# Plain fp32 matmuls in place of split fp32r products in a one-core transformer step

## What is computed

```
mod = silu(cond) @ w_mod + b_mod            # 2 conditioning vectors, 2048 x 12288, split into 6 parts
h   = rmsnorm(x) * (1 + sc_m) + sh_m
u   = h @ w_in                              # 384 x 2048 x 5120
m   = concat(A diff attention, B gated recurrence, C neighbourhood attention, D grouped attention)(u)
x   = x + g_m * rmsnorm(m @ w_out)          # 384 x 2048 x 2048
h   = rmsnorm(x) * (1 + sc_f) + sh_f
a,g = split(h @ w_ffn_in)                   # 384 x 2048 x 11264
x   = x + g_f * rmsnorm((silu(g) * a) @ w_ffn_out)   # 384 x 5632 x 2048
```

## Time and profile before

| what | value |
|---|---|
| median of 3 runs | 2067.38 us (2067.26 to 2074.31) |
| profiled execution, its span | 2065.1 us |
| profiled execution, its own time | not given beside the span |
| TensorE busy | 1910.1 us, 92% |
| VectorE busy | 1047.9 us, 51% |
| ScalarE busy | 857.6 us, 42% |
| HBM read | 311.54 MB |
| mean granted TensorE clock over the span | 0.969 of full |

### The profile page before, as it was taken

The page is one execution under the profiler, slowest core; times in us unless marked ns, Lnnn a source line. Parts: engine busy times, 40 slices in busy tenths (PEclk is TensorE's granted clock), DMA queues, the critical chain, the costliest instruction groups (busy, mean ns, idle before and its releaser), DMA issues.

```text
span 2065.1 us, 23115 instructions
## 1 busy us (share of the span) xinstructions
PE 1910.1 (92%) x8491; PEld 1460.6 (71%) x8491; DVE 1047.9 (51%) x1289; ACT 857.6 (42%) x1167; POOL 157.4 (8%) x225
## 2 busy tenths in 40 slices
PE   3889999999996779959999999999999989999995
PEld 1348666666664558848888888888888878888884
DVE  4883675866667743446233332333333345555553
ACT  4663555556555543333232322323223234444542
POOL 2000102410007700000000000000000000000000
PEclk8999999999998889979999999999999999999998
DMA  8873666666654023324333333333333343333321
GB/s 288 318 284 123 232 219 252 224 252 232 247 214 147 6 102 122 122 97 148 123 122 122 133 112 141 122 123 129 118 138 122 122 164 135 129 123 123 123 102 61
DMA packets 45028, 320.91 MB, mean 155 GB/s; under 512 B 5436, under 2 KB 5816, under 8 KB 7144
## 3 DMA queue, kind: packets, MB, share of 16 engines
q1 hardware_dynamic: 41216, 297.95, 39.5%
q0 software_dynamic: 3152, 18.93, 2.7%
q10 hardware_dynamic: 600, 3.21, 0.4%
HBM read 311.54 MB, written 8.52 MB: 155 GB/s over the span
## 4 chain that ended last, share of the span: by engine, by line
PE 83%; DVE 8%; ACT 3%; issue 2%; DMA 2%; DVEq 0%; ACTq 0%; POOL 0%; SPq 0%
PE ps L632 24%; PE ps L634 24%; PE ps L633 24%; DVE wlo L898 3%; PE ps L617 3%; PE ps L618 2%; ACT whi L279 1%; DMA raw<-in_weights 1%; PE ps L645 1%; DVE smalls L1112 1%; DMA rows<-in_state_rglru 1%; PE ps L847 1%; PE ps L773 1%; DVE x_sb L1203 1%; PE ps L796 1%
## 5 line engine op out<-in xcount | busy, mean ns | idle before, releaser
L898 DVE TENSOR_TENSOR wlo<-raw,whi 128x1024 fp32r<-128x1024 f32 x568 | 689.5, 1243 | 743.4 <-ACT whi L279 741.5
L279 ACT ACTIVATE whi<-raw 128x1024 fp32r<-128x1024 f32 x568 | 582.8, 1056 | 788.1 <-PE ps L634 753.1
L632 PE MATMUL ps<-whi,h_hi 128*128 128x512 f32 x1728 | 682.2, 395 | 18.8 <-DVE wlo L898 11.8
L634 PE MATMUL ps<-wlo,h_hi 128*128 128x512 f32 x1728 | 673.8, 390 | 0.0
L633 PE MATMUL ps<-whi,h_lo 128*128 128x512 f32 x1728 | 673.3, 390 | 0.0
L632 PEld LDWEIGHTS ps<-whi,h_hi 128*128 128x128 f32 x1728 | 324.9, 188 | 97.7 <-DVE wlo L898 22.4
L633 PEld LDWEIGHTS ps<-whi,h_lo 128*128 128x128 f32 x1728 | 325.0, 188 | 68.1 <-issue 1.7
L634 PEld LDWEIGHTS ps<-wlo,h_hi 128*128 128x128 f32 x1728 | 324.8, 188 | 68.3
L632 PE MATMUL ps<-whi,j_hi 128*128 128x512 f32 x528 | 209.7, 397 | 5.4 <-DVE j_lo L1253 3.9
L633 PE MATMUL ps<-whi,j_lo 128*128 128x512 f32 x528 | 206.1, 390 | 0.0
L634 PE MATMUL ps<-wlo,j_hi 128*128 128x512 f32 x528 | 206.1, 390 | 0.0
(11 more groups left out here) (204 smaller groups left out, 1033.0 us busy)
## 6 DMA issues: line engine op xcount, KB each, us to landing
raw<-in_weights SPq DMA_DIRECT2D x284, 1024.0 KB, 4.8
x_dram<-x_sb POOLq DMA_DIRECT2D x1, 3072.0 KB, 9.1
x_sb<-x_dram POOLq DMA_DIRECT2D x1, 3072.0 KB, 10.7
out<-x_sb POOLq DMA_DIRECT2D x3, 1024.0 KB, 4.7
x_sb<-in_x_sample ACTq DMA_DIRECT2D x1, 2048.0 KB, 15.0
x_sb<-in_x_sample POOLq DMA_DIRECT2D x1, 2048.0 KB, 9.4
x_sb<-in_x_prompt ACTq DMA_DIRECT2D x1, 1024.0 KB, 5.0
gw<-in_lru_gate_w POOLq DMA_DIRECT2D x4, 256.0 KB, 3.3
```

The lines of the kernel that those rows point to most:

```text
L279: nc.scalar.activation(whi[:, s % RING * 2 + b], raw[:, s, HK * b:HK * b + HK], ACT.Copy)\
L632: nc.tensor.matmul(acc, xh[:, kk + HK * b, xs], wh[:, kk, :], start=(k == 0), stop=False)
L634: ins = nc.tensor.matmul(acc, xh[:, kk + HK * b, xs], wl[:, kk, :], start=False, stop=(k == k_last))
L898: nc.vector.tensor_tensor(wlo[:, s % RING * 2 + b], raw[:, s, HK * b:HK * b + HK], whi[:, s % RING * 2 + b].bitcast(F32), ALU.subtract).th ...
```

## The change

1. All fp32r buffers, splits and their semaphores go. A matmul is plain fp32 on the raw weight tile and on unsplit activations (`hT`, `h3T`, `stat`). ScalarE and VectorE no longer touch weights.
2. `proj_tile` is 12 plain fp32 matmuls: tokens stationary, 512 weight columns moving. It serves the input projection, the output projection and the second FFN product.
3. `mod_tile` has the weights stationary: 16 plain fp32 matmuls, each with a 128x128 block of the tile loaded and two columns moving. The result lies in columns, so `rows_out`, `mod_select` and `cols_out` go; VectorE adds the bias on its way out of PSUM (`mod_out`).
4. The first FFN product has the weights stationary too. A tile is now 128 output columns x 2048 rows (`chunk`), 16 plain fp32 matmuls with 384 token columns moving. The result is already transposed: `h3_transposes` and `ht_out` go, and the work is in 44 pairs of tiles.
5. The ring has 10 tiles, and a slot is free once TensorE has used it. The residual stays in SBUF; both copies through DRAM go.
6. All loops over registers are written out.

```diff
-RAW = 4
-RING = 2
-HK = KG // 2
+RAW = 10
...
-C_F2 = C_F1 + 2 * FFN_N * KG
+C_F2 = C_F1 + 2 * FK
...
@@ sync
-            with sp.Fori(1, N_TILES // RAW) as i:
-                for s in range(RAW):
-
-                    sp.wait_ge(w_lo, i * (2 * RAW) + (2 * (s + 1) - 2 * RAW))
-                    sp.dma_start(raw[:, s].rearrange("p k n -> p (k n)"), wst[i * RAW + s]).then_inc(raw_in[s], 16)
+            for t in range(N_TILES):
+                if t >= RAW:
+                    sp.wait_ge(w_used, t - RAW + 1)
+                sp.dma_start(raw[:, t % RAW].rearrange("p k n -> p (k n)"), wst[t]).then_inc(raw_in[t % RAW], 16)
...
@@ tensor
-            def mod_tile(t, s, kg, bank):
-
-                for b, wh, wl in halves(t, s):
-                    for kk in range(HK):
-                        k = KG * kg + HK * b + kk
-                        nc.tensor.matmul(ps[bank][0:4, :], stat[:, k, :], wh[:, kk, :], start=(k == 0), stop=False)
-                        ins = nc.tensor.matmul(ps[bank][0:4, :], stat[:, k, :], wl[:, kk, :],
-                                               start=False, stop=(k == KD - 1))
-                    ins.then_inc(w_used, 1)
...
+            def mod_tile(t, kg, n):
+
+                tile_in(t)
                 for f in range(4):
+                    for kk in range(KG):
+                        k = KG * kg + kk
+                        ins = nc.tensor.matmul(ps[6 + n % 2][:, 2 * f:2 * f + 2], raw[:, t % RAW, kk, f * P:(f + 1) * P],
+                                               stat[:, k, :], start=(k == 0 and f == 0), stop=(k == KD - 1),
+                                               skip_group_check=True)
+                ins.then_inc(w_used, 1)
...
-                            nc.tensor.matmul(acc, xh[:, kk + HK * b, xs], wh[:, kk, :], start=(k == 0), stop=False)
-                            nc.tensor.matmul(acc, xl[:, kk + HK * b, xs], wh[:, kk, :], start=False, stop=False)
-                            ins = nc.tensor.matmul(acc, xh[:, kk + HK * b, xs], wl[:, kk, :],
-                                                   start=False, stop=(k == k_last))
...
+            def proj_tile(t, kg, bank, x, k_last, ready=None):
+
+                tile_in(t)
+                for kk in range(KG):
+                    k = KG * kg + kk
+                    if ready is not None:
+                        pe.wait_ge(h_f, ready + k + 1)
                     for tb in range(TB):
+                        ins = nc.tensor.matmul(ps[bank + tb][:, :], x[:, k, tb * P:(tb + 1) * P], raw[:, t % RAW, kk, :],
+                                               start=(k == 0), stop=(k == k_last))
+                ins.then_inc(w_used, 1)
...
+            def up(t, k, bank):
+
+                return nc.tensor.matmul(ps[bank][:, 0:T], raw[:, t % RAW, k // KG, k % KG * P:(k % KG + 1) * P], hT[:, k, :],
+                                        start=(k == 0), stop=(k == KD - 1))
...
+            for f in range(1, FK):
                 for part in range(2):
+                    t, bank = C_F1 + 2 * f + part, 2 * (f % 4) + part
...
+                    if f >= 4 and part == 0:
+                        pe.wait_ge(h3_ok, f - 3)
+                    tile_in(t)
+                    for k in range(KD):
+                        ins = up(t, k, bank)
+                    ins.then_inc(w_used, 1)
...
@@ vector
+            def mod_out(n):
+
+                dve.wait_ge(w_used, mod_done(n))
+                V.tensor_tensor(modc[:, 4 * n:4 * n + 4, :], ps[6 + n % 2][:, 0:8].rearrange("p (f j) -> p f j", j=2),
+                                pc1[:, 32 + 4 * n:36 + 4 * n].unsqueeze(2).to_broadcast([P, 4, 2]), ALU.add).then_inc(mod_col, 1)
...
+            for f in range(FK):
+                bg, ba = ps[2 * (f % 4)], ps[2 * (f % 4) + 1]
+                dve.wait_ge(s_tanh, f + 1)
+                link(V.scalar_tensor_tensor(sg[f % 2][:, :], sg[f % 2][:, :], 1.0, bg[:, 0:T], ALU.add, ALU.mult))
+                dve.wait_ge(w_used, C_F1 + 2 * f + 2)
+                V.scalar_tensor_tensor(h3T[:, f, :], sg[f % 2][:, :], 0.5, ba[:, 0:T], ALU.mult, ALU.mult).then_inc(h3_ok, 1)
...
@@ gpsimd
-            pool.dma_start(x1_dram, x_sb[:, :, :]).then_inc(spill, 16)
-            pool.wait_ge(ht_ps, 4 * FFN_N + 1)
-            pool.wait_ge(spill, 16)
-            pool.dma_start(x_sb[:, :, :], x1_dram).then_inc(x1_in, 16)
```

More of the change, by code:

```diff
@@ L109, in build @@
     rows_st = at("rows_st", [8, P], X0 + 19968)
-    sg = at("sg", [P, TB, NC], X0)
-    h3 = at("h3", [P, TB, NC], X0 + 6144)
     raw = at("raw", [P, RAW, KG, NC], RW0)
[L114 to L121, removed]
+    hT = at("hT", [P, KD, T], H0)
+    y2 = at("y2", [P, TB, D], H0)
     ppad = at("ppad", [GRID_W, 4 * NA_RHO, PADW], H0)
@@ L271, in _ @@
         @block.scalar
         def _(act):
[L273 to L283, removed]
@@ L357, in _ @@
[L357 to L365, removed]
@@ L414, in element @@
+            for m in range(N_EL):
+                i, e = m // 2, m % 2
+                u_out(m + 1)
                 if e == 0:
@@ L661, in _, with x_transpose @@
+            def x_transpose(k, done):
+                for tb in range(TB):
+                    ins = nc.tensor.transpose(ps[xt_bank(k, done)][:, tb * P:(tb + 1) * P], xn[:, tb, k * P:(k + 1) * P],
+                                              ident[:, :])
+                ins.then_inc(xt_ps, 1)
             pe.wait_ge(par_in, 64)
@@ L685, in _, with gate @@
                 for kg in range(KG):
-                    h_tile(C_IN0 + 4 * n + kg, kg % RING, kg, 3 * n, 0 if n == 0 else None)
-            def element(i, e, first):
-                n = i * 4 + (MOD1 + 2 * e)
-                pe.wait_ge(acc_free, i * 2 + (1 + e))
+                    proj_tile(C_IN0 + 4 * n + kg, kg, 3 * n, hT, KD - 1, 0 if n == 0 else None)
+            def gate(g):
+                d, kind = g % 2, g // 2
+                nc.tensor.matmul(ps[g % 3][:, 0:LW], gw[:, 2 * d + kind, :], XC[:, 0:LW], start=True, stop=True)\
+                    .then_inc(l_gate, 1)
+            for m in range(N_EL):
+                i, e = m // 2, m % 2
+                pe.wait_ge(acc_free, m + 1)
                 if e == 1:
                     pe.wait_ge(l_xp, i + 1)
-                elif not first:
+                elif m:
                     pe.wait_ge(l_tanh, i * 4)
-                for q, (what, m, kg) in enumerate(EL_PLAN):
-                    t, s = tile_no(i, e, q), q % RING
+                for q, (what, half, kg) in enumerate(EL_PLAN):
                     if what == "in":
-                        h_tile(t, s, kg, in_banks(e))
+                        proj_tile(tile_no(m, q), kg, 3 * e, hT, KD - 1)
                     else:
+                        n = MOD1 + 2 * m + half
                         if kg == 0:
-                            pe.wait_ge(mod_col, n + (m - 1))
-                        mod_tile(t, s, kg, 6 + m)
-                    if q == 0 and not first:
-                        mod_select(i * 4 + (MOD1 + 2 * e - 1), 7)
-                    if q == 6:
-                        mod_select(n, 6)
+                            mod_free(n)
+                        mod_tile(tile_no(m, q), kg, n)
                     if q == 2 and e == 1:
@@ L723, in element @@
                         ins.then_inc(l_tr, 1)
-            def gate(g):
-                d, kind = g % 2, g // 2
-                nc.tensor.matmul(ps[g % 3][:, 0:LW], gw[:, 2 * d + kind, :], XC[:, 0:LW], start=True, stop=True)\
-                    .then_inc(l_gate, 1)
-            for e in range(2):
-                element(0, e, e == 0)
-            with pe.Fori(1, N_EL // 2) as i:
-                for e in range(2):
-                    element(i, e, False)
-            mod_select(MOD_N - 1, 7)
             pe.wait_ge(acc_free, IN_N)
@@ L850, in ffn_in @@
-            def ffn_in(j, first):
-                for part in range(2):
-                    if not first:
-                        pe.wait_ge((s_silu, h3_ok)[part], j)
-                    for kg in range(KG):
-                        h_tile(j * 8 + (C_F1 + 4 * part + kg), kg % RING, kg, 3 * part, KD if first and part == 0 else None)
-                        if part == 0 and first and kg < 2:
-                            x_transposes(range(4 * kg + 8, 4 * kg + 12), KD)
-                        if part == 0 and not first and kg in (1, 2):
-                            h3_transposes(j - 1, kg - 1)
@@ L861, in _ @@
[L861 to L881 removed]
+            for k in range(5):
+                x_transpose(k, KD)
@@ L922, in _ @@
             V.scalar_tensor_tensor(spt[:, 0:8], pc2[:, LL:LL + 8], -1.0, pc2[:, LL:LL + 8], ALU.mult, ALU.max).then_inc(sp_a, 1)
-            for q in range(4):
-                lo_at(q)
             dve.wait_ge(sp_e, 1)
@@ L1232, in hidden @@
[L1232 to L1258 removed]
+            modulate(KD, SC_F, SH_F, True)
@@ L1470, in weight_tiles @@
     for t, (w, n, kg) in enumerate(order):
-        out[t] = tile(w, n, kg)
```

(1 more changed line is left out.)

649 lines of the change are left out of this document (186 added, 463 removed).

## The result

| what | before | after |
|---|---|---|
| median | 2068.52 us (4 runs) | 2759.79 us (4 runs, 2748.44 to 2764.79) |
| ratio after to before | | 1.3317, 95% interval 1.3278 to 1.3356 |
| span of the profiled execution | 2065.1 us | 2753.2 us (its own time 2754.95) |
| mean granted TensorE clock | 0.969 | 0.903 |

What follows compares the result with a forecast made beforehand. TensorE was taken as the bound, with the splits beside it. Stages of 247, 822, 119, 171, 27, 914, 461.5 and 22 sum to 2784 us, forecast 2786; own range 2740 to 2880, 8 in 10 range 2520 to 2880.

Steps and rivals of the forecast that it cites:

- Its 18.8 us: All waits of the high x high matmuls before the change, so the splits lie almost wholly beside TensorE.
- A projection tile: Input and output projections, FFN: plain fp32 takes 10.33 us instead of 8.19, losing 2.14 us on each of 188 tiles.
- A modulation tile: Opening and elements: 32 records at 0.213 us slow or 0.115 fast, TensorE setting the pace; slow in the opening.
- 664: Input projection and elements without the clock's part: projection tiles, 64 modulation tiles at 3.68 us, gates, transposes and slow start.
- 158: Elements: the clock's cost in us, about 4.9 a group over 32 groups, in a range of 0 to 298.
- The 3.5 us: Elements: how long the fast clock lasts into a group's modulation loads; the remaining 3.9 us take 1.85 times as long.
- Attention: Attention stage: with its 24 splits of 0.29 us gone, 119 us instead of 128.7, a gain of 10.
- rival 1: Opening and elements: the fast clock holds through full-block loads; opening 149 us, kernel 2530 us; chance 0.14.
- rival 2: Clock slow in the opening only, two modulation tiles being too short to bring it down; 2628 us; chance 0.07.
- rival 3: Elements: the clock doesn't recover inside a projection tile; second stage 1263 us, kernel 3230 us; chance 0.03.
- rival 4: Modulation tiles: instruction issue is the limit, each 0.05 us more per record costing 154 us; chance 0.02.
- rival 5: Projection and FFN tiles: a plain fp32 record in a long stream costs one pass, not two; 1870 us; chance 0.02.

Runs made afterwards that it cites:

- the grouped run: Changed kernel with each element's four projection tiles first, then its eight modulation tiles, one switch instead of four; 2816.41 us.

## Why the prediction was right

**The bound.** TensorE's time per tile decided every stage but attention, norm and tail. The splits were beside it, as the earlier trace rows said: taking away 595 of the 690 us of the low split was worth 41 us. The prediction's reading of the waits was too small, though. Its 18.8 us belong to one group of high x high matmuls. The same page has two more groups that waited, mostly for splits, which makes 45.8 us in all:

```profile
L632 PE MATMUL ps<-whi,j_hi 128*128 128x512 f32 x528 | 209.7, 397 | 5.4 <-DVE j_lo L1253 3.9
...
L617 PE MATMUL ps<-whi,stat 128*4 128x512 f32 x384 | 155.9, 406 | 21.6 <-DVE wlo L898 19.9
```

**A projection tile.** 10.33 us forecast from two records 0.43 apart and six gate records. The second FFN product measured 460.5 - 8 x 0.87 = 453.5 us for 44 tiles, 10.31 each, and the first 912.5 us for 88 with its transposes and start. A price read from a few records held for the 4256 records of the output projection and the FFN, in streams of up to 900 us, with weights stationary or tokens stationary alike. For the 960 records of the input projection it held where the clock stayed up (412 us in the run with 128 columns); in the changed kernel they took 471. Over 188 tiles the price is 400 us of the 691, and the run with plain fp32 in one product alone shows it without the rest of the change.

**A modulation tile.** The sum has 6.82 us slow and 3.68 fast: 32 records at the 0.213 and 0.115 us of the selection matmuls with 4 rows loaded. Measured 6.8 and 3.57, or 0.213 and 0.112 us a record: with 128 rows loaded a record costs the same as with 4. Which level holds, the runs show for both cases: 192 loads in a row with two columns behind each stayed at the slow one (0.213 us each in the grouped run), and the same loads with 128 columns behind each ran fast after the first 25 (0.112 us each).

At the fast clock the new form of a modulation tile still costs more than the old: 3.57 us against 8 x 0.2274 = 1.82 for its eight fp32r matmuls. In the opening, where DMA set the pace before (398 GB/s), little of that shows (143.7 us with 128 columns against 136.7); in the elements it is 64 x 1.75 = 112 us. No run kept the old form, conditioning vectors stationary and 512 columns moving, in plain fp32. By the price of 0.43 us a record it would be 8 x 0.43 = 3.4 us a tile in a dense stream, an estimate that no run here tests.

**The sizes.** The largest miss is the clock in the elements. Forecast 664 without it and 158 for it. The run with 128 columns shows 654 without it, in part since a record is 0.112 and not 0.115 us; so the clock's part is 794 - 654 = 140 us, 4.4 a group instead of 4.9. The rest of the 28 us too much is the 664. That 158 came so near 140 is partly luck, for its two parts missed in opposite ways. Added up from start to start and compared with the run with 128 columns, the loads cost 68 us more, 2.1 a group where 3.3 was forecast, and the projection tiles 59, 1.8 a group where 1.5 was; the rest lies in gates and transposes. The 3.5 us for which the loads were to stay fast was a guess from one place in the earlier trace rows; in the 32 groups the slow spacing began 2.3 to 5.6 us into the loads. Attention gained 5 us, not 10. TensorE's waits for the splits there were 10.3 us before (9.0 in 8 waits for `h_lo` at L1142, 1.3 at L1163), just the gain forecast; but the stage now begins with 6.7 us of waiting for the cached keys and 5.1 for the recurrence's last product, where it began with 3.3 us of waiting before. What makes up the difference is open. The opening was 4 us shorter than forecast.

**The rivals.** The fast clock doesn't hold with two columns (rival 1 would have been 2530 us; the run with 128 columns, in which it does hold, took 2514). It falls in the elements too (rival 2), and recovers inside a projection tile, in 12 to 13 us against 20.7 (rival 3). Issue isn't the limit: the same instruction stream ran a record every 0.112 us (rival 4). Plain fp32 was no cheaper in long streams (rival 5): 0.43 us for 512 columns in the second FFN product.

None of these versions comes near the kernel before. The best, with 128 columns, is 1.22 times as long, 446 us more. By the prices above about 400 us are the plain fp32 of the 188 tiles, 112 the form of the modulation tiles in the elements and 7 the opening; the waits, selections, hidden transposes and other work that went give some 70 back. That sum is an estimate.

## What to carry to other kernels

Work on an engine that is not the bottleneck can be nearly free, as 595 us of splits were worth 41 here; before taking it away, price what the bound engine does instead. Here three fp32r matmuls cost 0.68 us and the one plain fp32 matmul that replaces them 0.86.

A stretch of weight loads with little moving behind them ran at half of TensorE's clock here, with 2 and with 32 columns (granted 0.50, 0.213 us a record instead of 0.112), and what followed paid too: in the elements shown the first records of a projection tile are 0.85 us apart, the later ones 0.43. More columns moving cost nothing here, since a record with a load of 128 columns takes 0.112 us at the fast level with 2, 64 or 128 of them, and 128 gave back 245 us. With 64 columns it mattered what ran before: the same loads were slow ahead of the transposes (0.213 us each) and fast behind them (0.112).

Read such prices from the rows at both clock levels. A small helper of the old kernel, 192 records of selection, held the price of a third of the loss.

## What the runs showed that I had not expected

- With 64 moving columns behind each load the clock stayed at the fast level for 747 us, projection tiles among them, but did not rise in 54.7 us. With 128 it rose after 25 records; with 32 it neither rose nor stayed.
- 128 columns of plain fp32 hide wholly behind a load of 128 columns: the record takes 0.112 us with 64 columns and with 128 (85.87 and 85.92 us for 768).
- The clock column can hide a slow start. The record of the granted clock begins with the first rise, 25.0 us into the run with 128 columns and 76.9 us into the changed kernel; before that only the spacing of the matmuls, 0.213 or 0.112 us, shows the level.
- A ring of 4 in place of 10 cost 17 us without one wait for a tile, only through the clock (slow stretches of 369 us in all instead of 317). The executions of the changed kernel themselves differ by 16 us with its clock falling, and those of the run with 128 columns by 2.4. A difference of some 0.6% in a kernel with a repeating fall of the clock need not mean what it seems to.
